# First two score steps of two attentions issued ahead of the last gate tile; gate sigmoids in other scratch rows and banks

## The reference

```python
def even_layer(x, norm_g, w_in, b_f, gn_g, w_out):
    h = rms_norm(x, norm_g)
    q_f, k_f, v_f, f_l, q_r, k_r, v_r, z = jnp.split(h @ w_in, EVEN_SPLITS, axis=-1)
    o_f = fox_attention(q_f, k_f, v_f, f_l + b_f)      # 8 heads, softmax with a decay added to the scores
    o_r = retention(q_r, k_r, v_r) * gn_g              # 8 heads
    y = concatenate([o_f, o_r]) * jax.nn.silu(z)
    return x + y @ w_out

def odd_layer(x, norm_g, w_in, b_gate, ..., w_out):
    h = rms_norm(x, norm_g)
    q, kc, vc, ks, vs, kw, vw, gl, z = jnp.split(h @ w_in, ODD_SPLITS, axis=-1)
    o = nsa_attention(q, kc, vc, ks, vs, kw, vw, gl + b_gate, ...)   # 16 heads: compressed, selected and window branch
    return x + (o * jax.nn.silu(z)) @ w_out
```

## Time and profile before

| | |
|---|---|
| median of 3 runs | 1566.25 us |
| the profiled execution | 1566.48 us |
| its span | 1564.7 us |
| TensorE matmul busy | 1476.0 us (94%) |
| VectorE busy | 973.4 us (62%) |
| ScalarE busy | 882.0 us (56%) |
| mean granted TensorE clock | 0.981 |

### The profile page before, as it was taken

The page is one execution under the profiler, slowest core; times in us unless marked ns, Lnnn a source line. Parts: engine busy times, 40 slices in busy tenths (PEclk is TensorE's granted clock), DMA queues, the critical chain, the costliest instruction groups (busy, mean ns, idle before and its releaser), DMA issues.

```text
span 1564.7 us, 24980 instructions
## 1 busy us (share of the span) xinstructions
PE 1476.0 (94%) x10148; PEld 947.0 (61%) x10148; DVE 973.4 (62%) x1946; ACT 882.0 (56%) x1247; POOL 67.6 (4%) x148
## 2 busy tenths in 40 slices
PE   6999998999989999999998999989699999899997
PEld 3444485665458448585787666445385755466676
DVE  6732547888478566555667224576756336699974
ACT  4544456777554665454553453657354557678862
POOL 0000000000100100000010000001000000000000
PEclk8999999999999999999999999999899999999999
DMA  6233232111422334433325366411023332200002
GB/s 183 87 102 108 87 103 81 55 55 54 156 86 82 129 108 122 119 112 108 108 87 76 97 91 96 94 54 32 21 88 105 117 108 81 81 1 2 2 12 85
DMA packets 127218, 132.07 MB, mean 84 GB/s; under 512 B 9760, under 2 KB 124192, under 8 KB 126976
## 3 DMA queue, kind: packets, MB, share of 16 engines
q1 hardware_dynamic: 124336, 119.59, 27.0%
q0 software_dynamic: 2768, 10.89, 2.0%
HBM read 128.38 MB, written 2.10 MB: 83 GB/s over the span
## 4 chain that ended last, share of the span: by engine, by line
PE 59%; DVE 8%; ACT 4%; issue 2%; DMA 2%; POOL 0%; ACTq 0%; DVEq 0%
PE bank L709 8%; PE bank L710 8%; PE bank L711 8%; PE bank L748 6%; PE bank L750 5%; PE bank L749 5%; PE bank L942 3%; PE bank L924 3%; PE bank L915 2%; DVE wring L1872 2%; PE bank L911 1%; ACT whigh L1274 1%; DMA wring<-in_even_w_in 1%; PE bank L824 1%; DVE scr L2399 1%
## 5 line engine op out<-in xcount | busy, mean ns | idle before, releaser
L709 PE MATMUL bank<-xT,whigh 128*128 128x512 f16 x960 | 366.1, 381 | 10.4 <-DVE xT L2045 7.7
L710 PE MATMUL bank<-xT,whigh 128*128 128x512 f16 x960 | 366.0, 381 | 0.0
L711 PE MATMUL bank<-xT,wring 128*128 128x512 f16 x960 | 365.6, 381 | 0.0
L1872 DVE SCALAR_TENSOR_TENSOR wring<-wring,wsc,whigh 128x2048 f16<-128x2048 f32 x105 | 245.0, 2334 | 165.6 <-ACT whigh L1274 165.1
L1274 ACT ACTIVATE whigh<-wring,wsc 128x2048 f16<-128x2048 f32 x105 | 208.8, 1988 | 156.4 <-DVE wsc L1775 138.0
L1291 ACT ACTIVATE whigh<-wring 128x2048 bf16<-128x2048 f32 x105 | 199.0, 1895 | 121.3 <-DMA wring<-in_even_w_in 43.5
L748 PE MATMUL bank<-whigh,slab 128*128 128x256 f16 x800 | 218.0, 273 | 3.0 <-DVE wring L1872 1.2
L750 PE MATMUL bank<-whigh,slab 128*128 128x256 f16 x800 | 218.1, 273 | 0.0
L749 PE MATMUL bank<-wring,slab 128*128 128x256 f16 x800 | 218.0, 273 | 0.0
L709 PEld LDWEIGHTS bank<-xT,whigh 128*128 128x128 f16 x960 | 94.4, 98 | 126.3 <-DVE xT L2045 7.9
L711 PEld LDWEIGHTS bank<-xT,wring 128*128 128x128 f16 x960 | 94.4, 98 | 114.7 <-issue 2.5
(11 more groups left out here) (324 smaller groups left out, 2356.3 us busy)
## 6 DMA issues: line engine op xcount, KB each, us to landing
wring<-in_w_in SPq DMA_DIRECT2D x28, 1024.0 KB, 5.1
wring<-in_w_up SPq DMA_DIRECT2D x16, 1024.0 KB, 5.3
wring<-in_w_down SPq DMA_DIRECT2D x16, 1024.0 KB, 5.2
wring<-in_even_w_in SPq DMA_DIRECT2D x14, 1024.0 KB, 9.5
wring<-in_odd_w_in SPq DMA_DIRECT2D x14, 1024.0 KB, 4.9
wring<-in_w_a SPq DMA_DIRECT2D x4, 1024.0 KB, 5.2
wring<-in_w_out SPq DMA_DIRECT2D x4, 1024.0 KB, 5.2
wring<-in_even_w_out SPq DMA_DIRECT2D x4, 1024.0 KB, 4.7
```

The costliest lines, as they stand in the source:

```text
L709: pe.matmul(bank, wh[:, k, wcol:wcol + width], xh[:, k, :], start=k == 0, stop=False)
L710: pe.matmul(bank, wh[:, k, wcol:wcol + width], xl[:, k, :], start=False, stop=False)
L711: mm = pe.matmul(bank, wl[:, k, wcol:wcol + width], xh[:, k, :], start=False, stop=k == KC - 1)
L1872: dve.scalar_tensor_tensor(low_of(i)[:, :, 0:m], loaded(i)[:, :, 0:m], wsc[:, n:n + 1], high_of(i)[:, :, 0:m], ALU.mult, ALU.subtract).the ...
```

## The change

Steps 0 and 1 of each attention (`EARLY`) are issued ahead of gate tile 7 on TensorE, and behind tile 6's part on ScalarE and VectorE; the rest (`later`) follows where the whole attention stood. `attention(A)` becomes `attention(A, some)` on the three engines. On TensorE scores 0 and 1 wait for gate tile 5's eviction (`ze_ev`, `zo_ev` 6), since they write banks 0 to 3; ze therefore moves to `ZBANKS`, and its tile 2 waits for the last `vr` tile's eviction, which used to be waited for after tile 7. The sigmoids move from scratch rows 0 and 1 to rows 4 and 5, since the exponentials of steps 0 and 1 write rows 0 to 3. One semaphore (`sigmoid_made`) counts the sigmoids of `q`, `ze` and `zo`.

```diff
-                for i in range(N + VALUE_LAG):
+                for i in some:
...
-            feat("ze", 8, xhalves, SA)
+
+            def fox_start():
+                pe.wait_ge(s_("ze_ev"), n_("ze_ev", 6))
+                pe.wait_ge(s_("frow_both"), 1)
+                pe.wait_ge(s_("decay_in"), 32)
+                attention(FOX, EARLY)
+
+            feat("ze", 8, xhalves, ZBANKS, before={2: lambda: pe.wait_ge(s_("vr_ev"), n_("vr_ev", 8)), 7: fox_start})
             pe.wait_ge(s_("ze_ev"), n_("ze_ev", 8))
-            pe.wait_ge(s_("vr_ev"), n_("vr_ev", 8))
-            pe.wait_ge(s_("frow_both"), 1)
-            pe.wait_ge(s_("decay_in"), 32)
-            attention(FOX)
+            attention(FOX, FOX.later)
...
+            def nsa_start():
+                between_gates(7)
+                pe.wait_ge(s_("zo_ev"), n_("zo_ev", 6))
...
+                attention(NSA, EARLY)
+
+            feat("zo", 8, xhalves, ZBANKS, before={7: nsa_start, **{m: lambda m=m: between_gates(m) for m in range(1, 7)}})
             compressed_turn(7)
-            pe.wait_ge(s_("cs_ev"), 16)
             pe.wait_ge(s_("zo_ev"), n_("zo_ev", 8))
             pe.wait_ge(s_("ct_ev"), 16)
...
-            attention(NSA)
+            attention(NSA, NSA.later)
```

On ScalarE (zo alike, behind its tile 6):

```diff
-                act.activation(scr[:, m % 2, :], SA[m % 4][:, :], ACT.Sigmoid, scale=undo("ze", m // 2)).then_inc(s_("ze_sg"), 1)
+                act.activation(scr[:, 4 + m % 2, :], ZBANKS[m % 4][:, :], ACT.Sigmoid, scale=undo("ze", m // 2)).then_inc(s_("ze_sg"), 1)
                 act.wait_ge(s_("ze_sg"), own(s_("ze_sg")))
                 if m % 2 == 0:
                     following("ze", m // 2)
+                if m == 6:
+                    attention(FOX, EARLY)
...
             act.wait_ge(s_("ze_ev"), n_("ze_ev", 8))
-            attention(FOX)
+            attention(FOX, FOX.later)
```

On VectorE (zo alike):

```diff
+            def behind_even_gate(m):
+
+                if m >= 1:
+                    bound_behind("ze", m - 1)
+                if m == 6:
+                    attention(FOX, EARLY)
+
+            silu("ze", slab[5], ZBANKS, {m: lambda m=m: behind_even_gate(m) for m in range(8)})
+            bound_behind("ze", 7)
```

More of the change, by code:

```diff
@@ L342, in build @@
                 n += results
+        sigmoid_made = sem("sigmoid_made")
+        for i, stage in enumerate(("q", "ze", "zo")):
+            counted[stage + "_sg"] = sigmoid_made, 8 * i
         def s_(name):
@@ L470, in __init__ @@
                 self.steps = [(m, b, parts) for m in range(heads // 2) for b in range(branches) for parts in TILES]
+                self.later = range(2, len(self.steps) + 8)
             def q(self, h, t):
@@ L493, in y @@
                 return slab[5][:, m, :]
+        EARLY = range(2)
         FOX, NSA = Att("fox", 8, 1), Att("nsa", NH, 2)
@@ L897, in hgrn_ss, with attention @@
                 pe.matmul(SB[1][:, :], ones[:, :], scr[:, 3 + h % 2, :], start=True, stop=True).then_inc(s_("hg_ss"), 1)
-            def attention(A):
+            def attention(A, some):
                 n, steps, N = A.name, A.steps, len(A.steps)
-                for i in range(N + VALUE_LAG):
+                for i in some:
                     if i < N:
@@ L1571, in attention @@
                 highs = {VALUE_LAG + per * (m + 1) + 1: m for m in range(pairs)}
-                for i in range(max(highs) + 1):
+                for i in some:
                     if i in highs:
@@ L1593, in attention @@
                         ins.then_inc(s_(n + "_ex"), 1)
+            for m in range(8):
+                if m % 2 == 0:
+                    period("ze", m // 2)
+                act.wait_ge(s_("ze_mm"), n_("ze_mm", m + 1))
+                if m >= 2:
+                    act.wait_ge(s_("ze_ev"), n_("ze_ev", m - 1))
+                act.activation(scr[:, 4 + m % 2, :], ZBANKS[m % 4][:, :], ACT.Sigmoid, scale=undo("ze", m // 2)).then_inc(s_("ze_sg"), 1)
+                act.wait_ge(s_("ze_sg"), own(s_("ze_sg")))
+                if m % 2 == 0:
+                    following("ze", m // 2)
+                if m == 6:
+                    attention(FOX, EARLY)
             act.wait_ge(s_("ze_ev"), n_("ze_ev", 8))
-            attention(FOX)
+            attention(FOX, FOX.later)
             def ret_copies(m):
@@ L1746, in _ @@
                     act.wait_ge(s_("zo_ev"), n_("zo_ev", m - 1))
[L1747 removed]
+                act.activation(scr[:, 4 + m % 2, :], ZBANKS[m % 4][:, :], ACT.Sigmoid, scale=undo("zo", m // 2)).then_inc(s_("zo_sg"), 1)
                 act.wait_ge(s_("zo_sg"), own(s_("zo_sg")))
@@ L2339, in bound_behind, with attention @@
                 gate_bound(name, slab[5], row)
-            silu("ze", slab[5], SA, {m: lambda m=m: bound_behind("ze", m - 1) for m in range(1, 8)})
-            bound_behind("ze", 7)
-            def attention(A):
+            def attention(A, some):
                 n, steps, N = A.name, A.steps, len(A.steps)
@@ L2349, in attention @@
                 lows = {VALUE_LAG + per * (m + 1) + 2: m for m in range(pairs)}
-                for i in range(max(lows) + 1):
+                for i in some:
                     if i == 2:
```

15 lines of the change are left out of this document (8 added, 7 removed).

## The result

The change is slower. In the first comparison it took 1574.62 us (median of four executions, 1573.56 to 1576.91) beside 1566.22 before: ratio 1.0052, interval 1.0039 to 1.0065, or 8.4 us more (6.1 to 10.2). A second comparison, with twelve executions, gave 1571.61 beside 1566.67: ratio 1.0037 (1.0023 to 1.0051), 5.8 us more. The ratio is not that of the two medians, which are 4.9 us apart; where a time in microseconds is given against before, it comes from the ratio. The forecast was 4.6 us more, with a range that ended at 1573.8 us. The sign was right and the size too small.

What follows compares the result with a forecast made beforehand. TensorE bounds inside the attentions; at their starts it waits for VectorE and ScalarE until scores 4. Later scores 4 (0.4 + 1.9) and half clock (2.3) sum to 4.6 us more: 1570.9 us, range 1567.0 to 1573.8.

Steps and rivals of the forecast that it cites:

- Priming, even place: Way to scores 4 where gate ze ends and attention FOX begins: scores 4 start 0.4 us later, at 1042.03.
- Priming, odd place: Way to scores 4 where gate zo ends and attention NSA begins: scores 4 start 1.9 us later, at 1377.15.
- the price of the loads: ScalarE, both places: a table load costs its 1.28 us and nothing around it, against the skill's 2.66 us per switch.
- Edits that cost nothing: Both places: sigmoids in scratch rows 4 and 5, ze in other banks and the earlier vr wait add no time.
- The later release of SyncE's next slot: Out-projection slot released by tile 7 3.1 us later; used only after the attention, so no cost, else up to 3.1.
- Clock, even place: TensorE idle 4.8 us before scores 4 at ze/FOX, then half clock on scores 4 and later: 2.3 us, bounds 0 and 3.0.
- Clock, odd place: At zo/NSA, the slow stretch before covered only scores 2, 3 and transposes nothing late depended on; no term in the sum.
- rival B: Odd place: low clock outlasts the priming, full clock back a few us late, up to 2.5 us more: 1573.4; chance 0.10.
- A: Rival: the clock stays up at the even place, so only 2.3 us more: 1568.6; chance 0.27.
- C: Rival: silu 7 follows tile 7 as closely as before; scores 4 start 0.6 and 1.9 us earlier: 1563.8; chance 0.08.
- D: Rival: the change does nothing that counts, the primings being slack against something else: 1566.3; chance 0.04.
- E: Rival: each table switch costs the load's time once more as the pipeline drains, 5.1 us for four: 1576.0; chance 0.01.

Runs made afterwards that it cites:

- e3: The changed kernel with matmuls of no use in TensorE's idle stretches at both places, behind the last gate tile and ahead of scores 4: 2.5 us above before.
- e6: The changed kernel with tile 7's sigmoid replaced by a copy at both places, so no table swap back: 1567.20 us, 4.4 us below the change.
- f1: The changed kernel with both early parts put back, keeping other banks, scratch rows, earlier vr wait and split loops: 1566.12 us beside 1567.36 before, ratio 0.9990.
- e1: The changed kernel with the odd place put back in the order of before, the even place kept as changed: 2.7 us more than before.
- e7: The changed kernel with exps 0 and 1 put behind sigmoid 7 and step 0's normalizing behind bound 7: 1.7 us faster than before.

## Why the prediction was partly right

- **Priming, even place** (forecast +0.4): +0.3. The reduction costs 0.50 and the third load 1.28, as counted. Silu 7 comes 1.5 us behind tile 7 instead of 1.8, and scores 4 come 10.04 us behind silu 7 instead of 9.94. Right.
- **Priming, odd place** (+1.9): +2.1 against the profile of before in four executions of the change and +1.7 in one; against the other profiles with the odd place in the order of before it is 0.4 less. Idle 5.76 us before scores 2 (5.8 forecast). Right within that. Both together were confirmed by e3 (2.5 measured, 2.3 forecast), and the price of the loads by e6.
- **Edits that cost nothing**: right for the banks, the scratch rows and the earlier wait for vr, by f1. The later release of SyncE's next slot was not tried by itself; the two places account for the loss without it.
- **Clock, even place** (+2.3, bounds 0 and 3.0): +1.6. The mechanism was right, the picture was not: of two idle stretches, 2.6 and 4.8 us, I let only the second bring a fall. In truth the clock fell already after 2.3 us idle, came back under scores 3, and fell again after 3.2. The size, half of some 4 to 6 us, should have been half of 3.4.
- **Clock, odd place: the step that failed.** The forecast says of the kernel before that the slow stretch "covered just scores 2, 3 and transposes of which nothing late depended", and left the odd place's clock out of the sum. Its own numbers had the gap of 2.7 us behind them, and rival B priced the clock coming back late at up to 2.5 us with a chance of 0.10. What happens is a second fall, and it costs 1.6 to 4.7 us, 3.2 in the mean of the five profiles (16.0 / 5). Put in its place the sum would be 2.4 + 1.6 + 3.2 = 7.2 us, between the two comparisons (8.4 and 5.8). With the filling of e3, whose profile has no half clock at the two places, 2.5 us are left.
- **Rivals.** A fell: no profile of the change kept the clock. That is not a certainty of the order, since in e1, with the even place alone, the one profile kept it behind scores 4. B was right in its place and wrong in its mechanism and size. C fell on silu 7's start, as stated; e7 shows that it comes true when the exps do not stand ahead of sigmoid 7. D fell by the times, and by e3, in which the priming alone costs 2.5 us. E fell by e6: what looked like its size (1576.0) was clock.

## What to carry to other kernels

Work moved ahead of a phase's last tile leaves the engine that did it with nothing to do behind that tile: count not only when the next step starts but every idle stretch that the new order opens on TensorE, each as a possible fall to half clock, and ask what runs under it; where that is work on the path it costs half its length, and the length differs between executions. On ScalarE, moving one function ahead of the last use of another adds two table loads; leaving ScalarE's exponentials where they were and moving only TensorE's and VectorE's parts early gave a gain (1.7 us) and needed none of the loads. Where TensorE must wait and then is the bound, a few matmuls of no use can be worth about as much as the reordering itself (here 2.8 us were gained without them and 6.1 with them, in two comparisons whose intervals just overlap). They are to be tried and not assumed: in the kernel before, the same filling went with 3.1 us more.

## What the runs showed of the hardware

- The granted clock fell behind idle stretches of 2.3 and 3.2 us, while the 3.49 us before scores 2 had left it up in one execution; the same order in f1 fell there (half clock from 1038 to 1045, scores 4 one us later). In e1 3.23 us left it up, where 3.24 in the change brought a fall. Between 2.2 and 3.5 us no length of idle time seen here decided by itself.
- At the two places half clock lasted 3.4, 6.8 or 10.2 us in these profiles; the cost on work that bounds was half of what lay on it (1.6 us for 3.4).
- With two idle stretches of 2 to 6 us and a burst of work between them, the clock fell twice: all five profiles of the change show it at both places, while e1, with the even place in the same order, shows one fall there. The Trainium skill (TensorE: Matmul & The Clock Gate, section HAM oscillation — how this bites in real kernels) describes a kernel that waits between bursts of matmuls and starts every burst at half clock. The five profiles agree with that pattern, and e1 does not.
- Executions of one kernel differ by more than the terms that were forecast: the change ran from 1567.6 to 1579.2 us in one comparison, before from 1564.1 to 1571.8. The clock at the odd place is part of it (3.2 us, 33.76 against 30.61 in the table, between the shortest and the longest slow stretch). A single profile shows one draw, so the first one's 10.2 us of half clock was not the whole story; what stays open is what makes the odd place's slow stretch 3.4 us in one execution and 10.2 in the next.
